# Gate and up slabs as seven block products, with sums of weights by adding DMAs and VectorE, and a down projection in three parts

## The chip, the cores and the metric

The kernel runs on one core of a Trainium2 chip. A core has TensorE (PE, matrix products into the accumulators of PSUM, eight banks), VectorE (DVE), ScalarE (ACT), GpSimd (POOL), and SyncE (SP), which here only issues DMAs. Each engine works through its own list of instructions in order and waits for the others on semaphores. The metric is the device time of one execution in microseconds; lower is better.

## What is computed

One layer of a decoder for 520 tokens (512 of a prompt and 8 that are decoded), width 1024. A feed-forward block stands before and after the mixing part; the change concerns these two blocks ("FFN a" and "FFN b" below). The hidden width is 2816, which is 22 chunks of 128.

```python
D_FF = ((8 * D_MODEL // 3 + 127) // 128) * 128      # 2816

def _swiglu(x, w_gu, w_down):
    gate, up = jnp.split(x @ w_gu, 2, axis=-1)
    return (jax.nn.silu(gate) * up) @ w_down

h = _layernorm(ALPHA * x + 0.5 * _swiglu(x, p['ffa_w_gu'], p['ffa_w_down']), p['ln1_g'], p['ln1_b'])
...
mix = jnp.concatenate([o_da, o_rw], axis=-1) @ p['w_out']
h = _layernorm(ALPHA * h + mix, p['ln2_g'], p['ln2_b'])
y = _layernorm(ALPHA * h + 0.5 * _swiglu(h, p['ffb_w_gu'], p['ffb_w_down']), p['ln3_g'], p['ln3_b'])
```

## The kernel before

Features lie on the 128 partitions and tokens in the columns, so x is 8 chunks (`DC`) of 128x520. Float32 products are made from two parts in the fast format fp32r: a value w is split into w_hi (a rounded copy, by ScalarE) and w_lo = w - w_hi (by VectorE), and each product is hi·hi + hi·lo + lo·hi. So every weight tile of 128x128 costs three matmuls for each half (260 columns) of the tokens.

A **slab** is the weights of one output chunk: 8 tiles of 128x128 for gate and up. It costs 8 tiles x 3 x 2 halves = 48 matmuls of 128x260 (`multiply_slab`, line 298). SyncE loads two slabs at a time, 1 MB, into one of two buffers `RAW` (line 257) when both slabs that lay there are split. ScalarE's `split_high` (line 272) and VectorE's `split_low` (line 279) fill one of four places `WH`/`WL`. Each slab accumulates in one of four sets `acc` of two banks.

`gate_up` is a loop: each pass takes two gate slabs and two up slabs, 4 x 48 matmuls. While TensorE does one pass, ScalarE and VectorE split the slabs of the next (`ahead`), and turn the finished accumulators into two chunks of the hidden vector: silu (line 345), the product (358), and its split into `HH` and `HL` (348, 361). There are 11 passes for the 22 chunks, 2112 matmuls.

`down_tensor` multiplies the whole hidden vector with the down weights: 8 output chunks, each over 22 tiles in four slabs of 6, 6, 5 and 5 tiles (`DOWN_K`), 1056 matmuls. `residual` adds 2·ALPHA·x, taken from its two parts. A LayerNorm follows: its sums are taken by TensorE between the last slabs, and its last chunks become ready one by one while the next stage's first slabs are multiplied (`multiply_halved`, line 854, in FFN b).

TensorE is given work by hand in this order: FFN a, the input projection, the mixing (attention and the recurrent part), the output projection, FFN b. GpSimd has nothing to do in either FFN until the four additions for the norm.

## Time and profile before

| | us |
|---|---|
| median of 3 runs | 1302.99 |
| lowest, highest | 1302.15, 1303.44 |
| span of the profiled execution, first to last instruction | 1303.2 |
| TensorE busy, matmuls | 1253.9 (96%) |
| VectorE busy | 561.9 (43%) |
| ScalarE busy | 422.7 (32%) |
| GpSimd busy | 89.1 (7%) |
| mean granted clock of TensorE | 0.991 |

The profile is of one execution. Its span ends within 0.3 us of the median, so a sum made on the span holds for the median. "Busy" adds up the rows of an engine, and matmul rows overlap each other: the pace of matmuls is read from a stretch and its number of matmuls, not from one row's length. In the same way rows of VectorE and ScalarE can overlap by about 0.1 us, so what an instruction occupies is read from the starts of two that follow each other without idle time.

### The profile page before, as it was taken

How to read it: one execution, taken by the hardware profiler on the slowest of the kernel's cores; microseconds unless marked ns; L12 is line 12 of the kernel's file. 1: busy time of each engine (PE TensorE's matmuls, PEld its weight loads, DVE VectorE, ACT ScalarE, POOL GpSimd, SP SyncE). 2: the span in 40 equal slices, each digit the busy share in tenths (PEclk: the TensorE clock that was granted, in tenths of full speed). 3: DMA queues.
4: the chain of work that ended last, by engine and by line, in shares of the span. 5: the costliest groups of instructions: out<-in, count | busy, mean ns of one | idle time of the engine just before them, and what ended most of it. 6: DMA issues, size and time to landing. Idle time of an engine off the chain costs nothing.

```text
span 1303.2 us, 30892 instructions
## 1 busy us (share of the span) xinstructions
PE 1253.9 (96%) x13258; PEld 1135.4 (87%) x13258; DVE 561.9 (43%) x851; ACT 422.7 (32%) x679; POOL 89.1 (7%) x89
## 2 busy tenths in 40 slices
PE   9999999999999999998878888999999999999996
PEld 8999999999998998886446445698999999999996
DVE  4323333223437543354654544787533333323253
ACT  4222222221223513433543334333422222222223
POOL 0000000000100110000450011010000000000021
PEclk9999999999999999999989999999999999999998
DMA  6222222222222666645644899641222222222221
GB/s 228 98 97 75 86 97 97 69 87 92 83 93 100 243 199 243 223 146 182 210 167 144 283 309 300 244 166 66 98 93 72 93 97 97 80 65 90 90 65 67
DMA packets 57847, 176.96 MB, mean 136 GB/s; under 512 B 7313, under 2 KB 7570, under 8 KB 49426
## 3 DMA queue, kind: packets, MB, share of 16 engines
q1 hardware_dynamic: 54578, 169.48, 38.6%
q10 hardware_dynamic: 3168, 6.02, 1.3%
q8 instruction: 78, 1.28, 0.4%
q14 instruction: 23, 0.19, 0.0%
HBM read 164.64 MB, written 10.83 MB: 135 GB/s over the span
## 4 chain that ended last, share of the span: by engine, by line
PE 86%; DVE 5%; issue 2%; ACT 2%; DMA 2%; POOL 1%; SPq 1%; ACTq 0%; DVEq 0%; POOLq 0%
PE acc L298 66%; PE acc L854 3%; PE acc L1612 2%; PE acc L1682 2%; PE acc L321 2%; PE acc L1164 1%; PE acc L1877 1%; PE acc L545 1%; PE acc L1869 1%; PE acc L1854 1%; PE acc L424 1%; PE acc L1188 1%; DMA scratch<-early_gates 1%; PE acc L411 1%; PE acc L1957 1%
## 5 line engine op out<-in xcount | busy, mean ns | idle before, releaser
L279 DVE TENSOR_TENSOR weights_lo<-weights_raw,weights_hi 128x1024 fp32r<-128x1024 f32 (+2 forms) x184 | 206.6, 1125 | 519.9 <-ACT weights_hi L272 519.8
L272 ACT ACTIVATE weights_hi<-weights_raw 128x1024 fp32r<-128x1024 f32 (+2 forms) x184 | 177.5, 966 | 540.9 <-PE acc L298 519.7
L298 PE MATMUL acc<-x_hi,weights_hi 128*128 128x260 f32 x1696 | 345.0, 285 | 0.1
L298 PE MATMUL acc<-x_hi,weights_lo 128*128 128x260 f32 x1696 | 342.2, 283 | 0.0
L298 PE MATMUL acc<-x_lo,weights_hi 128*128 128x260 f32 x1696 | 342.0, 283 | 0.0
L298 PEld LDWEIGHTS acc<-x_hi,weights_hi 128*128 128x128 f32 x1696 | 262.3, 189 | 12.9 <-issue 11.9
L298 PEld LDWEIGHTS acc<-x_hi,weights_lo 128*128 128x128 f32 x1696 | 262.1, 189 | 0.0
L298 PEld LDWEIGHTS acc<-x_lo,weights_hi 128*128 128x128 f32 x1696 | 261.5, 189 | 0.0
L298 PE MATMUL acc<-hidden_hi,weights_hi 128*128 128x260 f32 x684 | 139.0, 284 | 0.0
L298 PE MATMUL acc<-hidden_hi,weights_lo 128*128 128x260 f32 x684 | 137.7, 283 | 0.0
L298 PE MATMUL acc<-hidden_lo,weights_hi 128*128 128x260 f32 x684 | 137.6, 283 | 0.0
L298 PEld LDWEIGHTS acc<-hidden_hi,weights_hi 128*128 128x128 f32 x684 | 105.4, 188 | 0.9
L298 PEld LDWEIGHTS acc<-hidden_lo,weights_hi 128*128 128x128 f32 x684 | 105.5, 188 | 0.0
L298 PEld LDWEIGHTS acc<-hidden_hi,weights_lo 128*128 128x128 f32 x684 | 105.5, 188 | 0.0
L684 POOL TENSOR_TENSOR scratch<-y_sum 128x520 f32<-128x520 f32 x3 | 5.1, 1698 | 785.2 <-DVE y_sum L449 785.2
L348 ACT ACTIVATE hidden_hi<-scratch 128x520 f32 (+1 forms) x44 | 28.1, 639 | 85.8 <-DVE scratch L358 85.8
L361 DVE TENSOR_TENSOR hidden_lo<-scratch,hidden_hi 128x520 f32 (+1 forms) x44 | 30.8, 700 | 38.9 <-ACT hidden_hi L348 38.9
L1612 PE MATMUL acc<-cache_pages,query_columns 128*32 128x512 f32 x256 | 34.9, 618 | 0.0
L854 PE MATMUL acc<-x_hi,weights_hi 128*128 128x260 f32 x128 | 30.8, 298 | 3.1 <-ACT x_hi L728 1.5
L358 DVE TENSOR_TENSOR scratch<-scratch,acc 128x520 f32<-128x520 f32 x44 | 30.3, 690 | 0.0
L1854 PEld LDWEIGHTS acc<-level_y,inverse_turned 64*64 64x64 f32 x768 | 13.5, 135 | 18.2 <-issue 15.7
L854 PE MATMUL acc<-x_hi,weights_lo 128*128 128x260 f32 x128 | 29.2, 285 | 0.0
(352 smaller groups left out, 1352.8 us busy)
## 6 DMA issues: line engine op xcount, KB each, us to landing
cache_pages<-in_cache_k SPq DMA_DIRECT2D x128, 256.0 KB, 3.6
weights_raw<-in_gate_up_b SPq DMA_DIRECT2D x22, 1024.0 KB, 4.8
weights_raw<-in_gate_up_a SPq DMA_DIRECT2D x21, 1024.0 KB, 4.8
cache_pages<-in_cache_v SPq DMA_DIRECT2D x64, 256.0 KB, 3.6
weights_raw<-in_w_in SPq DMA_DIRECT2D x13, 1024.0 KB, 5.8
projected<-in_cache_v SPq DMA_DIRECT2D x48, 256.0 KB, 3.7
weights_raw<-in_down_a SPq DMA_DIRECT2D x8, 768.0 KB, 4.1
weights_raw<-in_down_b SPq DMA_DIRECT2D x8, 768.0 KB, 4.2
```

The source lines that it names most:

```text
L272: nc.scalar.activation(WH[pr.slot(k)][:, 0:nk, :], RAW[slot][:, 0:nk, P * (k % 2):P * (k % 2) + P], ACT.Copy).then_inc(split_hi, 1)
L279: nc.vector.tensor_tensor(WL[pr.slot(k)][:, 0:nk, :], RAW[slot][:, 0:nk, P * (k % 2):P * (k % 2) + P], WH[pr.slot(k)][:, 0:nk, :].bitcast( ...
L298: mm = nc.tensor.matmul(acc[s][:, a, 0:HALF], w[slot][:, t, :], x[:, k0 + t, HALF * a:HALF * a + HALF], start=begins and t == tiles[0] and ...
L321: mm = nc.tensor.matmul(acc[s][:, a, 0:HALF], w[slot][:, t, :], x[:, t, HALF * a:HALF * a + HALF], start=seen[k] == 1 and m == 0, stop=see ...
L348: nc.scalar.activation(HH[:, bass.ds(2 * (i - 1) + k - 2, 1), :], SCR[:, k:k + 1, :], ACT.Copy).then_inc(h_hi, 1)
L358: dve.tensor_tensor(halves(SCR[:, k, :]), halves(SCR[:, k - 2, :]), accv(k), ALU.mult).then_inc(hidden, 1)
L361: dve.tensor_tensor(HL[:, bass.ds(c, 1), :], SCR[:, k:k + 1, :], HH[:, bass.ds(c, 1), :].bitcast(f32), ALU.subtract).then_inc(acc_free[k], 1)
L411: mm = nc.tensor.matmul(out[32 * q:32 * q + 32, :], MEAN[:, 0:32], x[:, t:t + EIGHTH], start=start, stop=stop)
L854: return nc.tensor.matmul(acc[s][:, h, 0:HALF], w[pr.slot(k)][:, c, :], x[:, c, HALF * h:HALF * h + HALF], start=c == 0 and m == 0, stop=c ...
L1612: mm = nc.tensor.matmul(bank(DECODE_BANK)[32 * h:32 * h + 32, :], QZ[:, h, b, :], PG[k % RING_GROUPS][:, :, P * h:P * h + P], start=b == 0 ...
L1682: mm = nc.tensor.matmul(bank(DECODE_BANK)[32 * j:32 * j + 8, :], WZ[:, n, 8 * b:8 * b + 8], page(N_GROUPS + k, j), start=False, stop=k == ...
L1854: mm = nc.tensor.matmul(two_banks(name)[64 * q:64 * q + 64, r, 64 * k:64 * k + 64], flat(lhs)[rows, cols], flat(rhs)[rows, cols], start=Tr ...
```

## The change

**Seven products.** Of the 22 pairs (gate chunk, up chunk) of each FFN the first two (`PLAIN`) are multiplied as before. Each of the other 20 is seen as a product of 2x2 blocks: the weights as gate or up times the two halves of the 1024 inputs (four quarters of 128x512), x as two halves of the inputs times two halves of the tokens. Such a product is made of seven block products in place of eight, four of them with sums of quarters of weights and of x. One block product is 4 tiles x 3 matmuls = 12 matmuls into one bank (`product_tensor`), a pair 84 where it was 96.

**Sums of x.** Once for each FFN, while TensorE multiplies the two plain pairs, VectorE makes four sums of x of 128x1040 and their low parts, and ScalarE their high parts (`x_sum_vector`, `x_sum_high`, `x_sum_low`). In FFN b x itself lacks its bias in the float32 copy, so ScalarE first makes eight passes of 128x520 (`plain_x_scalar`), which wait until the norm is done. The hidden vector's products use `Y` for the residual, too.

**Sums of weights.** For pair j the three quarters that are used alone are split in one step each (`outer_high`, `outer_low`, 128x1536). The four sums lie in a buffer `SUMS[j % 2]`. SyncE loads two quarters there a second time (2 x 256 KB beside the 1 MB). VectorE writes the two others as sums (`outer_sums_vector`, 128x2x512), and then GpSimd issues two DMAs that add 256 KB within SBUF: [1] += [0], and, after it has landed, [3] += [1] (`whole_sums_pool`). Both must have landed before ScalarE and VectorE split the sums, in two steps of 128x1024 each (`sums_high`, `sums_low`).

**Combining.** The seven results go through ScalarE and VectorE: `first_scalar` (128x260), `second_vector`, `third_vector` (128x260), `ends_vector` (128x520), `gates_vector` (128x780), silu (128x520), `hidden_vector` (128x520), `hidden_high` and `hidden_low`.

**Down in three parts.** The hidden vector is made in groups of 7, 7 and 8 chunks (the first two of them plain), and after each group the down projection over these chunks follows: 8 slabs of 7, 7 or 8 tiles, each result added to `Y` by VectorE (`down_added_vector`). The number of matmuls, 1056, is the same. The last group's slabs are followed by the norm in the order that the output projection had (`out_tensor`, `out_scalar`, `out_vector`). The loops are written out.

The core of the diff:

```diff
-DOWN_K = (6, 6, 5, 5)
+GROUPS = (7, 7, 8)
+GROUP_AT = (0, 7, 14)
+PLAIN = 2
...
+class Sevens:
...
+    ORDER = (1, 6, 7, 5, 2, 4, 3)
...
-DOWN_BODY = [(sum(DOWN_K[:r]), DOWN_K[r], sets, r == 0, r == 3) for sets in ((0, 1), (2, 3)) for r in range(4)]
+DOWN_BODY = [[(0, n, (0, 1), True, True), (0, n, (2, 3), True, True)] for n in GROUPS]
...
+        def plain_x_scalar(act):
+            act.wait_ge(x_ready, DC + 22)
+            for c in range(DC):
+                bias = VEC[:, V_LN + 3 * DC + c:V_LN + 3 * DC + c + 1]
+                nc.scalar.activation(Y[:, c, :], Y[:, c, :], ACT.Identity, bias=bias).then_inc(g("x_passes"), 1)
+        def x_sum_vector(dve, u, n):
+            out = XS[:, n, :, :]
+            if u:
+                dve.wait_ge(g("x_passes"), 4 + DC)
...
+        def outer_sums_vector(dve, sv, j):
+            dve.wait_ge(raw_ready[sv.raw_slot(j)], sv.raw_count(j))
+            raw, to = raw_quarters(sv, j), sums_of(sv, j)
+            two = to[:, :, :].rearrange("p (a b) n -> p a b n", b=2)[:, :, 0, :]
+            nc.vector.tensor_tensor(two, raw[:, 0:2, :], raw[:, 3:4, :].broadcast_to([P, 2, 4 * P]), ALU.add).then_inc(g("summed"), 1)
+        def whole_sums_pool(pool, sv, j):
+            to = sums_of(sv, j)
+            pool.wait_ge(raw_ready[sv.raw_slot(j)], sv.raw_count(j))
+            pool.wait_ge(g("summed"), sv.pair(j) + 1)
+            pool.dma_start(to[:, 1, :], to[:, 0, :], accum_op=ALU.add).then_inc(whole_sums(j), 16)
+            pool.wait_ge(whole_sums(j), whole_count(sv, j) - 16)
+            pool.dma_start(to[:, 3, :], to[:, 1, :], accum_op=ALU.add).then_inc(whole_sums(j), 16)
...
+        def sums_high(act, sv, j, which):
+            at = SUM_AT[which]
+            act.wait_ge(whole_sums(j), whole_count(sv, j))
+            weights_room(act, sv, j)
+            n = 0 if which == "first" else 2
+            nc.scalar.activation(weights_set(j, HI)[:, at:at + 2, :], sums_of(sv, j)[:, n:n + 2, :], ACT.Copy).then_inc(g("parts_hi"), 1)
+        def sums_low(dve, sv, j, which):
+            at = SUM_AT[which]
+            dve.wait_ge(g("parts_hi"), part_done(sv, j, which))
+            n = 0 if which == "first" else 2
+            nc.vector.tensor_tensor(weights_set(j, LO)[:, at:at + 2, :], sums_of(sv, j)[:, n:n + 2, :],
+                                    weights_set(j, HI)[:, at:at + 2, :].bitcast(f32), ALU.subtract).then_inc(g("parts_lo"), 1)
...
+        def sevens_tensor(pe, u, sv, begins):
+            for j in range(sv.pairs):
+                for which in sv.ORDER:
+                    pe.wait_ge(g("parts_lo"), part_done(sv, j, PART_OF[which]))
+                    if begins and j == 0 and which in X_SUM:
+                        pe.wait_ge(g("x_steps"), x_step(u, "low", X_SUM[which]))
+                    if j == 0:
+                        s = BANK_OF[which] // 2
+                        pe.wait_ge(acc_free[s], sv.used0[s])
+                    elif which == 1:
+                        pe.wait_ge(g("evicted"), 2 * sv.pair(j) - 1)
+                    else:
+                        pe.wait_ge(g("combined"), combined_at(sv, j - 1, DRAINED_BY[which]))
+                    product_tensor(pe, sv, j, which)
...
+        def sevens_scalar(act, u, sv, begins, down):
+            last = sv.pairs - 1
+            for j in range(sv.pairs):
+                if j < last:
+                    outer_high(act, sv, j + 1)
+                if j:
+                    silu_scalar(act, sv, j - 1)
+                first_scalar(act, u, sv, j)
+                if j < last:
+                    sums_high(act, sv, j + 1, "first")
+                else:
+                    split_high(act, down, 0, 0)
+                if j:
+                    hidden_high(act, sv, j - 1, begins)
+                if j < last:
+                    sums_high(act, sv, j + 1, "last")
+                else:
+                    for k in (1, 2):
+                        split_high(act, down, 0, k)
+            silu_scalar(act, sv, last)
+            hidden_high(act, sv, last, begins)
+            split_high(act, down, 0, 3)
+        def sevens_vector(dve, u, sv, down):
+            last = sv.pairs - 1
+            for j in range(sv.pairs):
+                if j:
+                    gates_vector(dve, sv, j - 1)
+                if j < last:
+                    outer_low(dve, sv, j + 1)
+                if j:
+                    hidden_vector(dve, sv, j - 1)
+                second_vector(dve, sv, j)
+                if j < last:
+                    sums_low(dve, sv, j + 1, "first")
+                if j:
+                    hidden_low(dve, u, sv, j - 1)
+                third_vector(dve, sv, j)
+                if j == last:
+                    split_low(dve, down, 0, 0)
+                ends_vector(dve, sv, j)
+                if j < last - 1:
+                    outer_sums_vector(dve, sv, j + 2)
+                if j < last:
+                    sums_low(dve, sv, j + 1, "last")
+                else:
+                    for k in (1, 2):
+                        split_low(dve, down, 0, k)
+            gates_vector(dve, sv, last)
+            hidden_vector(dve, sv, last)
+            hidden_low(dve, u, sv, last)
+            split_low(dve, down, 0, 3)
+        def first_down_tensor(pe, u, sv, down, begins):
+            last = sv.pairs - 1
+            def part(t):
+                pe.wait_ge(h_ready, u * FC + sv.chunk0 + sv.pairs - down.body[0][1] + t + 1)
+            for k in range(down.slabs):
+                pe.wait_ge(g("combined"), combined_at(sv, last, ("second", "ends", "gates", "gates")[k]))
+                multiply_slab(pe, down, 0, k, HH, HL, part=part if k == 0 else None)
...
+        def feed_forward_vector(dve, up, u, sevens, downs):
+            sv = sevens[0]
+            x_sum_vector(dve, u, 0)
+            x_sum_vector(dve, u, 1)
+            outer_sums_vector(dve, sv, 0)
+            x_sum_vector(dve, u, 2)
+            x_sum_vector(dve, u, 3)
+            outer_low(dve, sv, 0)
+            sums_low(dve, sv, 0, "first")
+            plain_hidden_vector(dve, up, u, 0)
+            for n in (1, 2):
+                x_sum_low(dve, u, n)
+            plain_hidden_vector(dve, up, u, 1)
+            sums_low(dve, sv, 0, "last")
+            for n in (0, 3):
+                x_sum_low(dve, u, n)
+            for c in range(PLAIN):
+                plain_low_vector(dve, u, c)
+            outer_sums_vector(dve, sv, 1)
+            for n, (sv, down) in enumerate(zip(sevens, downs)):
+                sevens_vector(dve, u, sv, down)
+                if n < 2:
+                    nxt = sevens[n + 1]
+                    for k in range(down.slabs):
+                        down_added_vector(dve, down, 0, k, n == 0)
+                        split_low(dve, down, 1, k)
+                    outer_sums_vector(dve, nxt, 0)
+                    down_added_vector(dve, down, 1, 0, n == 0)
+                    outer_low(dve, nxt, 0)
+                    sums_low(dve, nxt, 0, "first")
+                    down_added_vector(dve, down, 1, 1, n == 0)
+                    sums_low(dve, nxt, 0, "last")
+                    outer_sums_vector(dve, nxt, 1)
+                    for k in (2, 3):
+                        down_added_vector(dve, down, 1, k, n == 0)
...
+            def load_pairs(sv, w):
+                for j in range(sv.pairs):
+                    raw_room(sp, sv.block0 + j)
+                    slot = sv.raw_slot(j)
+                    sp.dma_start(RAW[slot][:, :, :], w[sv.chunk0 + j, :, :].rearrange("p (k n) -> p k n", n=2 * P))\
+                        .then_inc(raw_ready[slot], 16)
+                    wait_from_one(sp, g("parts_lo"), 3 * (sv.pair0 if j < 2 else sv.pair(j - 1)))
+                    for n in (1, 2):
+                        sp.dma_start(sums_of(sv, j)[:, 2 * n - 1, :], w[sv.chunk0 + j, :, 4 * P * n:4 * P * n + 4 * P])\
+                            .then_inc(raw_ready[slot], 16)
...
+            feed_forward_pool(pool, sevens_a)
             norm_pool(pool, 0)
...
+            plain_x_scalar(act)
+            feed_forward_scalar(act, up_b, 1, sevens_b, downs_b)
+            out_scalar(act, downs_b[-1], 2)
```

How the order moves. **VectorE, in the middle of gate and up.** Before, one pass (two chunks; the passes of the loop have the same steps):

```order
L279 TENSOR_TENSOR weights_lo0<-weights_raw0,weights_hi0 128x1024 [waits split_hi,tables_in]
L279 TENSOR_TENSOR weights_lo1<-weights_raw0,weights_hi1 128x1024 [waits split_hi]
L279 TENSOR_TENSOR weights_lo2<-weights_raw1,weights_hi2 128x1024 [waits split_hi]
L358 TENSOR_TENSOR scratch<-scratch,acc2 128x520 [waits slab_used,acc_free0]
L361 TENSOR_TENSOR hidden_lo<-scratch,hidden_hi 128x520 [waits h_hi]
L279 TENSOR_TENSOR weights_lo3<-weights_raw1,weights_hi3 128x1024 [waits split_hi]
L358 TENSOR_TENSOR scratch<-scratch,acc3 128x520 [waits slab_used,acc_free1]
L361 TENSOR_TENSOR hidden_lo<-scratch,hidden_hi 128x520 [waits h_hi]
```

After, one iteration j for one chunk (L652 is `gates_vector` of the pair before, L544 `outer_sums_vector` for the pair after the next, L589 and L579 the low parts for the next pair):

```order
L652 TENSOR_TENSOR scratch<-banks,scratch 128x780 [waits combined,product]
L589 TENSOR_TENSOR weights_lo<-weights_raw1,weights_hi 128x1536 [waits parts_hi]
L660 SCALAR_TENSOR_TENSOR scratch<-scratch 128x520 [waits evicted]
L634 TENSOR_TENSOR scratch<-banks,scratch 128x260 [waits evicted,product]
L579 TENSOR_TENSOR weights_lo<-summed_weights1,weights_hi 128x1024 [waits parts_hi]
L675 TENSOR_TENSOR hidden_lo<-scratch,hidden_hi 128x520 [waits h_hi]
L639 TENSOR_TENSOR scratch<-banks,scratch 128x260 [waits combined,product]
L645 TENSOR_TENSOR scratch<-banks,scratch 128x520 [waits combined,product]
L544 TENSOR_TENSOR summed_weights0<-weights_raw0 128x2x512 [waits raw_ready0]
L579 TENSOR_TENSOR weights_lo<-summed_weights1,weights_hi 128x1024 [waits parts_hi]
```

In place of two 1024-wide splits and two 520-wide steps for each chunk there are ten instructions. The first of the two L579 waits for parts of ScalarE that wait for both adding DMAs (`parts_hi` follows `whole_sums`), and everything behind it stands in VectorE's order, the next `outer_sums_vector` (L544) among it.

**ScalarE beside it**, after, one iteration (L573 is `sums_high`):

```order
L585 ACTIVATE more_weights_hi<-weights_raw0 128x1536 [waits product,raw_ready0]
L656 ACTIVATE scratch<-scratch 128x520 [waits combined]
L629 ACTIVATE scratch<-banks 128x260 [waits h_ready,product]
L573 ACTIVATE more_weights_hi<-summed_weights0 128x1024 [waits product,whole_sums0]
L670 ACTIVATE hidden_hi<-scratch 128x520 [waits combined]
L573 ACTIVATE more_weights_hi<-summed_weights0 128x1024 [waits product,whole_sums0]
```

The first L573 stands ahead of the hidden chunk's high part and waits for `whole_sums`.

**GpSimd and its DMAs.** Before, at the start of the program, GpSimd goes from its constants to the additions of the first norm:

```order
L2786 MEMSET epsilons 128x1 x5
L684 ISA
L684 TENSOR_TENSOR scratch<-y_sum 128x520 [waits early_centred]
L684 TENSOR_TENSOR scratch<-scratch,y_sum 128x520 [waits all_summed,early_centred] x2
```

After, from the same place (the first two pairs of 20 of FFN a):

```order
L3164 MEMSET epsilons 128x1 x5
L551 DMA summed_weights0<-summed_weights0 128x512 [waits summed,raw_ready0]
L553 DMA summed_weights0<-summed_weights0 128x512 [waits whole_sums0]
L551 DMA summed_weights1<-summed_weights1 128x512 [waits summed,raw_ready1]
L553 DMA summed_weights1<-summed_weights1 128x512 [waits whole_sums1]
```

The 20 pairs of DMAs stand where there was nothing; within a pair the second waits for the first to land, and the first for VectorE's sums (`summed`) and the loads. A pair of DMAs for j is issued while TensorE is at pair j-1 or j-2.

## Rows read from the trace of the kernel before

**Rows 1.** The page: the span, and the busy time of each engine.

```profile
span 1303.2 us, 30892 instructions
...
PE 1253.9 (96%) x13258; PEld 1135.4 (87%) x13258; DVE 561.9 (43%) x851; ACT 422.7 (32%) x679; POOL 89.1 (7%) x89
```

**Rows 2.** The chain of waits in order of time: start us, us, what; x matmuls.

```profile
15.50 324.68 PE acc L298 x2700
...
391.05 2.16 PE acc L545 x18
...
924.83 307.11 PE acc L298 x2556
```

**Rows 3.** Timeline of TensorE: start us, us, line, operation; two stage starts.

```profile
9.73 0.39 PE L298 MATMUL acc<-x_lo,weights_hi 128*128 128x260 f32 x2
...
924.67 0.40 PE L298 MATMUL acc<-x_hi,weights_hi 128*128 128x260 f32 x2
```

**Rows 4.** Windows: us, busy us (xcount) of PE, PEld, DVE, ACT, POOL; clock, DMA share, GB/s.

```profile
925.00:1232.00 307.00, 307.00 (x2557) 306.97 (x2556) 101.06 (x113) 81.36 (x102) 0.00 (x0) 1.00 0.28 91
...
1294.00:1296.00 2.00, 0.00 (x0) 0.00 (x0) 2.00 (x5) 1.24 (x3) 2.00 (x2) 0.54 0.44 164
```

**Rows 5.** Timeline of VectorE: durations, and starts of neighbours that follow without idle.

```profile
18.95 2.36 DVE L279 TENSOR_TENSOR weights_lo<-weights_raw,weights_hi 128x1024 fp32r<-128x1024 f32 x2 [3.50 <-ACT weights_hi L272]
...
103.46 1.23 DVE L279 TENSOR_TENSOR weights_lo<-weights_raw,weights_hi 128x1024 fp32r<-128x1024 f32 x1 [2.38 <-ACT weights_hi L272]
...
104.60 0.69 DVE L358 TENSOR_TENSOR scratch<-scratch,acc 128x520 f32<-128x520 f32 x1
...
392.96 0.43 DVE L483 TENSOR_TENSOR y_sum<-acc,y_sum 128x260 f32<-128x260 f32 x1 [1.17 <-PE acc L545]
...
393.30 1.22 DVE L279 TENSOR_TENSOR weights_lo<-weights_raw,weights_hi 128x1024 fp32r<-128x1024 f32 x1
...
883.11 0.70 DVE L456 SCALAR_TENSOR_TENSOR y_sum<-x_lo,y_sum 128x520 f32<-128x520 f32 x1
...
883.73 0.69 DVE L454 SCALAR_TENSOR_TENSOR y_sum<-x_hi,scratch 128x520 f32<-128x520 f32 x1
...
918.25 0.76 DVE L798 SCALAR_TENSOR_TENSOR x_lo<-y_sum,feature_vectors,x_hi 128x520 fp32r<-128x520 f32 x1 [0.80 <-ACT x_hi L728]
```

**Rows 6.** Timeline of ScalarE: the table load, a 1024 copy, a silu, a 520 copy.

```profile
21.66 1.28 ACT L345 ACT_TABLE_LOAD   x1
...
108.07 1.06 ACT L272 ACTIVATE weights_hi<-weights_raw 128x1024 fp32r<-128x1024 f32 x1 [2.02 <-PE acc L298]
...
109.04 0.59 ACT L345 ACTIVATE scratch<-acc 128x520 f32<-128x520 f32 x1
...
99.59 0.64 ACT L348 ACTIVATE hidden_hi<-scratch 128x520 f32 x1 [1.99 <-DVE scratch L358]
```

**Rows 7.** The page: DMA issues, KB each, median us from issue to landing.

```profile
cache_pages<-in_cache_k SPq DMA_DIRECT2D x128, 256.0 KB, 3.6
...
weights_raw<-in_gate_up_b SPq DMA_DIRECT2D x22, 1024.0 KB, 4.8
```

**Rows 8.** The same for the whole program, further issues.

```profile
r_features<-in_cache_v SPq DMA_DIRECT2D x16, 256.0 KB, 4.0
...
out_y<-y_sum SPq DMA_DIRECT2D x8, 260.0 KB, 2.1
...
early_gates<-y_sum ACTq DMA_DIRECT2D x4, 260.0 KB, 2.4
```

**Rows 9.** Timeline of SyncE (SPq issues DMAs), first weight load of the loop.

```profile
15.62 20.38 SPq L257 DMA_DIRECT2D weights_raw<-in_gate_up_a  x4
```

**Rows 10.** Timeline of VectorE and GpSimd, a stretch in which both run.

```profile
349.95 0.96 DVE L279 TENSOR_TENSOR weights_lo<-weights_raw,weights_hi 128x768 fp32r<-128x768 f32 x1 [2.26 <-ACT weights_hi L272]
...
353.56 2.02 DVE L279 TENSOR_TENSOR weights_lo<-weights_raw,weights_hi 128x768 fp32r<-128x768 f32 x1 [1.43 <-ACT weights_hi L272]
...
353.44 1.32 POOL L684 TENSOR_TENSOR scratch<-scratch,y_sum 128x520 f32<-128x520 f32 x1
```

541 lines of the change are left out of this document (345 added, 196 removed).

## The prediction

> **What bounds the kernel now.** I read the page first: TensorE is busy for 1253.9 of 1303.2 us, VectorE for 561.9, ScalarE for 422.7 [rows 1]. The chain of waits shows that each FFN's gate-up and down matmuls are one piece without a gap: 2700 matmuls in 324.68 us and 2556 in 307.11 us [rows 2]. That is 0.1202 us for each in both, so an FFN lasts as long as its matmuls, and taking one away is worth 0.1202 us. In a window of FFN b VectorE works for 101 of 307 us, ScalarE for 81, and the granted clock is 1.00 [rows 4]. Where all matmuls of a stretch go into one bank, as in a block product, 18 take 2.16 us, the same pace [rows 2]. All further steps are times in which TensorE may have to wait in the new order.
>
> **What is removed.** 20 pairs in each FFN cost 84 matmuls for 96: 2 x 20 x 12 = 480, times 0.1202 = **57.7 us less**. One block product is 12 x 0.1202 = 1.44 us, a pair 10.10 us (11.54 before). The down matmuls are the same in number.
>
> **VectorE's steps.** 1024 wide it takes 1.23 us and frees the engine after 1.14 (103.46 to 104.60); 520 wide 0.70 and 0.62; 260 wide from PSUM 0.43 and 0.34 [rows 5]. From 520 to 1024 the slope is 1.05 ns a column, so 1536 costs 1.68, 780 from PSUM 0.88. An iteration (gates 0.88, outer low 1.68, hidden 0.62, second 0.34, first sums low 1.14, hidden low 0.62, third 0.34, ends 0.61, outer sums 1.14, last sums low 1.14) is 8.5 us, under 10.10: VectorE alone isn't the bound. ScalarE has two copies 1024 wide at 1.06, one 1536 wide at 1.49, two 520 and one 260, some 5.2 us [rows 6]. The norm tails and the split of the down slabs (1.2 us of VectorE in each slab of 5.05 us) hide behind matmuls as before; I take 0 for them, and 1 us in all if that fails.
>
> **The loop through the adding DMAs.** What can be longer than 10.10 us is a loop. Let D be the time from the end of the outer sums to the landing of the second adding DMA. From there follow ScalarE's high part (1.06), then on VectorE first sums low (1.14), hidden low (0.62), third (0.34), ends (0.61) and the next outer sums (1.23): with 0.1 for hand-overs the loop takes **P = D + 5.1**. Until D = 5.0 it hides behind a pair; above, each iteration is longer than a pair.
>
> D is not in the trace: GpSimd issues no DMA there. The nearest rows: 256 KB from HBM among other loads land after 3.6 us [rows 7], others after 4.0; 260 KB out of SBUF after 2.1 and 2.4 [rows 8]. The adding DMAs move between places in SBUF like the latter, but read the target too and run beside loads of 1 MB, which take 4.8 us [rows 7], like the former. So D lies between 2 x 2.4 = 4.8 and 2 x 4.0 + 0.2 = 8.2. I see no reason for either end and take the middle of 2.4 and 3.6, 3.0, with 0.1 for each hand-over: **D = 6.2**.
>
> The Trainium skill (DMA: Bandwidth & Descriptors, "Anatomy of one DMA — SWDGE (gpsimd) path") fits a DMA that GpSimd issues as 2.0 us plus bytes over 436 GB/s. By that, an estimate from the page, two of 256 KB are D = 5.2, and the sum below would give 1268; no row here shows such a DMA.
>
> **Cost in groups two and three.** The outer sums of pairs 0 and 1 are made during the down slabs and hide. Count from the group's first block product: the fourth product ends at 5.8, ends and outer sums for pair 2 at 7.65. Then high part and the rest of an iteration bring the last low part of pair 2 at 13.8 + D, and of the last pair p-1 at 13.8 + D + (p-3)(D+5.1) - 1.1. TensorE wants it for the third product of that pair, at 10.10(p-1) + 2.9. The difference is 5D - 30.4 for p = 7 and 6D - 35.4 for p = 8: 0.6 and 1.8 us at D = 6.2. For two FFNs: **4.8 us**.
>
> **Cost in group one** (5 pairs), where nothing was made ahead. FFN a: the block for pair 0 is asked for at 15.62 [rows 9]; VectorE is free of the plain slabs at 18.95 + 2.36 = 21.3 [rows 5], makes two sums of x (1.25 each) and the outer sums, which end at 24.9. High part at 26.0 + D; then on ScalarE a silu and three parts of x (0.5, 3 x 1.0), so the last low part of pair 0 at 31.8 + D. Behind it stand two low parts of x, two hidden parts and the outer sums of pair 1, at 36.4 + D. The last low part of pair 1 follows at 42.0 + 2D, of pair 4 three loops later at 56.2 + 5D, and five products after that the group ends: 63.4 + 5D. Without waits it would end 190 matmuls after 9.73 [rows 3] plus 5 x 10.10: 83.1. **Cost 5D - 19.7 = 11.3 us.** FFN b: x is whole at 918.25 + 0.76 = 919.0 [rows 5]; eight passes of ScalarE (0.64 long, 0.55 apart) [rows 6] end at 923.6, so the outer sums of pair 0 end at 927.3, 902.4 later than in FFN a, and the group at 965.8 + 5D. TensorE is through with the plain pairs at 924.7 already [rows 3], so without waits it would end at 975.2. **Cost 5D - 9.4 = 21.6 us.** (A table load of 1.28 [rows 6] lies in ScalarE's time before, ahead of D's end.) Even with D = 0 TensorE would wait 7.5 us there, since the outer high part comes only after x's passes.
>
> **The sum.** -57.7 + 11.3 + 21.6 + 4.8 = -20.0: 1303.2 becomes **1283**; the median of the runs is within 0.3 us of that span. With all groups waiting the change is 32D - 218.4, so it is zero at **D = 6.8**, and each 0.1 us of D costs 3.2 us.
>
> **Rivals.**
> - **Short DMAs.** D = 5.0, both near the 2.4 us row: groups two and three are free, group one costs 5.3 and 15.6: -36.8, 1266. For it: source and target in SBUF, no HBM. Against: they add, and loads run beside them. The page's fit above speaks for this one.
> - **The adding DMAs are the new bound, and the kernel is slower.** D = 7.7, two at the 3.6 us of the same size with 0.25 of hand-over each. The loop is 12.8 us, longer than the 11.54 of a pair before; +28, 1331. From D = 6.8 on this decides. For it: the row has the same size, and a weight load falls on the second DMA in each loop. In the trace VectorE and GpSimd hinder each other: the split that takes 0.96 alone takes 2.02 beside a GpSimd addition [rows 10]. Against: the row reads HBM. (By the Trainium skill, SBUF — State Buffer, "Who interferes with whom", a tensor_tensor of VectorE takes only the shared read port, so descriptor writing isn't held up; by that the hindrance in the row would be absent and D nothing longer. The row has a GpSimd read, so it doesn't contradict.)
> - **The clock falls in the waits.** At the end of the program the granted clock is 0.54 in a stretch in which TensorE has nothing to do [rows 4]. TensorE waits 7.5 us and more at the start of FFN b and several us in group one of both. If that costs one pair's time at half speed in each FFN, 2 x 10.1, the time is 1303, no change. Against: the forecast's waits are split over several products.
>
> **How the numbers follow.** Forecast (D 5.6 to 6.75) 0.42; short DMAs 0.15; slower 0.35; the clock, or D close to 6.8, 0.08. The measurement can tell about 0.2% (2.6 us) from no change. So faster 0.57, same 0.08, slower 0.35. The range goes from D = 4.8, -38.8 with 2 us off for what I rounded, 1262, to D = 8.2, +44, 1347: I give 1262 to 1345, which leaves out 0.1 at each end or less.
>
> **What would show it.** Right: the matmuls' pace stays 0.120 us; TensorE waits in FFN b's group one for about 20 us, most for weights' low parts; successive outer sums of one group are 11.3 us apart. A group of 5, 7 or 8 pairs in which the outer sums are 10.1 apart shows the short case, 12.5 and more the slower one. The issue-to-landing of the adding DMAs, near 3.0, is the number on which all hangs. The forecast is wrong if TensorE waits for anything else in groups two and three, if VectorE's steps there grow beside GpSimd's work, or if the granted clock in the FFNs falls below 1.

## The result

The changed kernel took **1462.57 us** (median of 4 runs, 1453.69 to 1468.94), the kernel before 1303.22 us beside it: a ratio of **1.121**, 95% interval 1.116 to 1.126. That is slower by 159 us. 1283 was forecast, and the range ended at 1345.

The page of the profile after, the same lines as in [rows 1], and with them the clock in 40 slices and the chain that ended last:

```profile
span 1466.0 us, 30172 instructions
...
PE 1259.5 (86%) x12778; PEld 1123.0 (77%) x12778; DVE 787.6 (54%) x1107; ACT 496.9 (34%) x759; POOL 158.6 (11%) x169
...
PEclk9899989999899999999999999997899899989898
...
PE 39%; DMA 29%; DVE 16%; issue 7%; ACT 5%; SPq 2%; POOL 1%; ACTq 0%; DVEq 0%; POOLq 0%
...
summed_weights<-summed_weights POOLq DMA_DIRECT2D x80, 256.0 KB, 4.5
```

TensorE has its 480 matmuls less (12,778 for 13,258), but the share of the span in which it works fell from 96% to 86%. Before, an FFN was one piece of TensorE in the chain [rows 2]. Now 29% of the chain are DMAs, and the page puts 26% down to `summed_weights<-summed_weights` alone, the 80 adding DMAs. They land after 4.5 us at the median; 3.0 was taken.

The chain of waits inside one group of FFN a (start us, us, what) shows the loop, one turn of it:

```profile
183.93 1.14 DVE summed_weights L544
...
185.11 0.49 issue
185.60 4.42 DMA summed_weights<-summed_weights
190.02 0.28 issue
190.31 5.35 DMA summed_weights<-summed_weights
...
195.68 1.07 ACT weights_hi L573
...
196.77 0.56 DVE weights_lo L579
197.33 0.58 issue
197.91 0.69 DVE hidden_lo L675
198.61 0.35 DVE scratch L639
...
199.05 0.70 DVE scratch L645
199.75 1.14 DVE summed_weights L544
```

From the end of the outer sums (183.93 + 1.14 = 185.07) to the high part (195.68) D is 10.6 us: 0.5 until the first adding DMA begins, 4.4 for it, 0.3, 5.35 for the second. The turn takes 199.75 - 183.93 = 15.8 us, and D + 5.1 = 15.7. So the loop is the one that the prediction drew, step by step; one term of it, D, had been taken 4.4 us too small.

Whom TensorE waits for (us in total, times, longest), kernel after:

```profile
PE banks L603 <- DVE more_weights_lo L579: 68.8, 32, 5.1
PE banks L603 <- DVE weights_lo L579: 67.9, 36, 5.6
PE banks L603 <- issue: 10.0, 2, 5.4
PE banks L603 <- DVE more_weights_lo L589: 8.2, 1, 8.2
```

L579 is the low part of the sums, the last link of the loop: 136.7 us in 68 waits. The 10.0 us to which the view gives no engine are one wait in the first pair of each FFN (4.6 and 5.4). The 8.2 us at L589 are the start of FFN b, put at 7.5.

### The profile page after: what moved, and what is told of

Its sections match the earlier page's. It is cut to its first block, busy times and chain, and to the rows that moved or that the text cites. A ratio compares the mean times of both kernels' runs of the same rounds, so it can differ in the third digit from the quotient of the medians.

```text
span 1466.0 us, 30172 instructions
## 1 busy us (share of the span) xinstructions
PE 1259.5 (86%) x12778; PEld 1123.0 (77%) x12778; DVE 787.6 (54%) x1107; ACT 496.9 (34%) x759; POOL 158.6 (11%) x169
## 4 chain that ended last, share of the span: by engine, by line
PE 39%; DMA 29%; DVE 16%; issue 7%; ACT 5%; SPq 2%; POOL 1%; ACTq 0%; DVEq 0%; POOLq 0%
DMA summed_weights<-summed_weights 26%; PE banks L389 20%; PE banks L603 3%; DVE summed_weights L544 3%; DVE more_weights_lo L579 2%; DVE scratch L645 2%; SPq L3073 2%; ACT more_weights_hi L573 2%; PE banks L1982 2%; PE banks L1239 1%; PE banks L412 1%; DVE hidden_lo L675 1%; ACT weights_hi L573 1%; PE banks L989 1%; PE banks L2052 1%
## 5 line engine op out<-in xcount | busy, mean ns | idle before, releaser
L603 PE MATMUL banks<-x_sums_hi,more_weights_hi 128*128 128x260 f32 x352 | 115.1, 327 | 78.8 <-DVE more_weights_lo L579 68.8
L368 DVE TENSOR_TENSOR weights_lo<-weights_raw,weights_hi 128x1024 fp32r<-128x1024 f32 (+1 forms) x82 | 96.8, 1187 | 118.5 <-ACT weights_hi L360 117.9
L603 PE MATMUL banks<-x_sums_hi,weights_hi 128*128 128x260 f32 x288 | 93.9, 326 | 67.9 <-DVE weights_lo L579 67.9
L579 DVE TENSOR_TENSOR more_weights_lo<-summed_weights,more_weights_hi 128x1024 fp32r<-128x1024 f32 x44 | 53.8, 1222 | 165.9 <-ACT more_weights_hi L573 165.9
L389 PE MATMUL banks<-hidden_hi,weights_hi 128*128 128x260 f32 x576 | 116.5, 283 | 0.0
L389 PE MATMUL banks<-hidden_hi,weights_lo 128*128 128x260 f32 x576 | 115.5, 282 | 0.0
L389 PE MATMUL banks<-hidden_lo,weights_hi 128*128 128x260 f32 x576 | 115.5, 282 | 0.0
L579 DVE TENSOR_TENSOR weights_lo<-summed_weights,weights_hi 128x1024 fp32r<-128x1024 f32 x36 | 44.0, 1222 | 130.3 <-ACT weights_hi L573 130.3
L573 ACT ACTIVATE more_weights_hi<-summed_weights 128x1024 fp32r<-128x1024 f32 x44 | 45.9, 1051 | 192.1 <-DMA summed_weights<-summed_weights 192.1
L603 PE MATMUL banks<-x_sums_lo,more_weights_hi 128*128 128x260 f32 x352 | 110.0, 312 | 0.0
L603 PE MATMUL banks<-x_sums_hi,more_weights_lo 128*128 128x260 f32 x352 | 109.8, 312 | 0.0
L603 PE MATMUL banks<-x_sums_lo,weights_hi 128*128 128x260 f32 x288 | 89.6, 311 | 0.0
L603 PE MATMUL banks<-x_sums_hi,weights_lo 128*128 128x260 f32 x288 | 89.6, 311 | 0.0
L573 ACT ACTIVATE weights_hi<-summed_weights 128x1024 fp32r<-128x1024 f32 x36 | 37.3, 1051 | 144.3 <-DMA summed_weights<-summed_weights 144.3
```

The source lines that it names most:

```text
L368: nc.vector.tensor_tensor(WL[pr.slot(i, k)][:, 0:nk, :], RAW[slot][:, 0:nk, P * (k % 2):P * (k % 2) + P], WH[pr.slot(i, k)][:, 0:nk, :].bi ...
L389: mm = nc.tensor.matmul(acc[s][:, a, 0:HALF], w[slot][:, t, :], x[:, k0 + t, HALF * a:HALF * a + HALF], start=begins and t == tiles[0] and ...
L573: nc.scalar.activation(weights_set(j, HI)[:, at:at + 2, :], sums_of(sv, j)[:, n:n + 2, :], ACT.Copy).then_inc(g("parts_hi"), 1)
L579: nc.vector.tensor_tensor(weights_set(j, LO)[:, at:at + 2, :], sums_of(sv, j)[:, n:n + 2, :], weights_set(j, HI)[:, at:at + 2, :].bitcast( ...
L603: mm = nc.tensor.matmul(product_bank(which), w[a][:, P * t:P * t + P], x[b], start=t == 0 and m == 0, stop=t == 3 and m == 2)
```

## The experiments

Times of the kernel before were 1306.6, 1306.5 and 1307.0 us in the three sets of runs (1299.46 to 1311.48); each ratio is against its own set. In what follows D is read for each of the 40 pairs, from the end of L544 to the first L573 after its second adding DMA, and averaged; in the kernel after it is 10.7 us on average (8.2 to 12.9).

**1. No adding DMA at all.** VectorE makes the third and fourth sum too, from the raw slab, and the second loads go.

```diff
             nc.vector.tensor_tensor(two, raw[:, 0:2, :], raw[:, 3:4, :].broadcast_to([P, 2, 4 * P]), ALU.add).then_inc(g("summed"), 1)
+            dve.wait_ge(g("summed"), n + 1)
+            nc.vector.tensor_tensor(to[:, 1, :], raw[:, 1, :], to[:, 0, :], ALU.add).then_inc(g("summed"), 1)
+            dve.wait_ge(g("summed"), n + 2)
+            nc.vector.tensor_tensor(to[:, 3, :], raw[:, 2, :], to[:, 1, :], ALU.add).then_inc(g("summed"), 1)
```

> All four sums of weights are made by VectorE; the adding DMAs and the second loads of two quarters are gone, the seven products stay. Theory L (the loop from outer sums through two adding DMAs, 10.5 us long, back to outer sums sets the time): nothing is left in that loop, VectorE's iteration grows from 8.5 by two steps 128x512 (0.6 each) to 9.8 us, still under the 10.1 of TensorE; the waits that stay are the starts of the FFNs (about 4 and 14 us) and 0 to 4 us in the groups; so 1303 - 58 + 17 to 22 = 1262 to 1275, successive outer sums of a group 10.1 to 10.6 apart, granted clock in the groups 1.00. Rival V (VectorE has too many steps per pair and its order is what TensorE waits for): more work for it makes it no faster than the changed kernel, above 1450. Rival S (seven products, their bank order or the down projection in three parts cost it): stays above 1330.

Measured: **1267.56 us**, ratio 0.9705 (0.967 to 0.974). VectorE's timeline in a group (start us, us; the lines are one further down than in the listing):

```profile
154.34 1.22 DVE L545 TENSOR_TENSOR summed_weights<-weights_raw 128x1024 f32<-128x1024 f32 x1
155.59 0.69 DVE L547 TENSOR_TENSOR summed_weights<-weights_raw,summed_weights 128x512 f32<-128x512 f32 x1
156.32 0.69 DVE L549 TENSOR_TENSOR summed_weights<-weights_raw,summed_weights 128x512 f32<-128x512 f32 x1
...
164.44 1.22 DVE L545 TENSOR_TENSOR summed_weights<-weights_raw 128x1024 f32<-128x1024 f32 x1
```

The two sums cost VectorE 1.4 us, and the outer sums stand 10.1 us apart, TensorE's own pace of 84 matmuls. So the loss lies in the way in which two sums are made, not in the block products. (The second loads went with the DMAs here; experiment 6 keeps both.)

**2. One adding DMA in place of two.** The third sum goes to VectorE, the fourth stays a DMA, and one of the two second loads goes.

```diff
-            pool.dma_start(to[:, 1, :], to[:, 0, :], accum_op=ALU.add).then_inc(whole_sums(j), 16)
-            pool.wait_ge(whole_sums(j), whole_count(sv, j) - 16)
             pool.dma_start(to[:, 3, :], to[:, 1, :], accum_op=ALU.add).then_inc(whole_sums(j), 16)
```

> One adding DMA for each pair instead of two: VectorE makes the third sum (128x512, 0.6 us), GpSimd adds only the fourth; one 256 KB load less. Theory L: D falls from 10.5 to 4.4 to 5.5 plus 0.5, about 5.6, the loop to 5.6 + 5.1 = 10.7 us, so by the sum 32D - 218 with D = 5.6 to 6 and 0.6 us less for VectorE: 1275 to 1300. Rival V: no faster than 1450. Rival B: half of the gap at most, above 1370.

Measured: **1281.45 us**, ratio 0.9822 (0.977 to 0.9874). The DMA lands after 4.2 us at the median; three successive outer sums stand 11.2 and 12.0 us apart (they start at 159.14, 170.35 and 182.39). In this order of VectorE one DMA of this kind nearly fits behind a pair, two don't.

**3. The same two DMAs, copying and not adding.** This leaves out the two additions.

```diff
-            pool.dma_start(to[:, 1, :], to[:, 0, :], accum_op=ALU.add).then_inc(whole_sums(j), 16)
+            pool.dma_start(to[:, 1, :], to[:, 0, :]).then_inc(whole_sums(j), 16)
```

> The two DMAs of GpSimd copy instead of adding, same bytes, same places, same waits (two of the four sums of weights are then not the sums; this leaves two additions out). If reading the target and adding makes the DMA long: landing 3.2 us and under instead of 4.4 and 5.3, D 7, time about 1340. If it is the queue, GpSimd's 0.86 us and the loads beside it: landing within 0.4 us of 4.4 and 5.3, time within 20 us of 1463.

Measured: **1364.67 us**, ratio 1.0447 (1.0396 to 1.0497). From the chain of waits, the same place as above:

```profile
182.19 2.40 DMA summed_weights<-summed_weights
...
184.87 5.32 DMA summed_weights<-summed_weights
```

Here the first falls from 4.42 to 2.40 us and the second stays at 5.3. Over all 40 pairs the first lands after 2.4 us at the median (4.4 when adding), the second after 4.6 (5.3), and D is 8.2 on average for 10.7. So adding itself is worth some 2.4 us of D, most of it in the first DMA; most of what the second takes has another cause. Neither of the two cases expected is met whole, and the time, 1365, lies between theirs.

**4. The order on VectorE.** The DMAs stay, but the outer sums of pair j+2 are made right after `second_vector` of pair j, one `sums_low`, `hidden_low`, `third` and `ends` earlier.

```diff
                 second_vector(dve, sv, j)
+                if j < last - 1:
+                    outer_sums_vector(dve, sv, j + 2)
                 if j < last:
                     sums_low(dve, sv, j + 1, "first")
...
-                if j < last - 1:
-                    outer_sums_vector(dve, sv, j + 2)
```

> Only one instruction of VectorE's order moves: outer sums for pair j+2 stand ahead of the first low part of the sums of j+1 (was: behind the ends), so they no longer wait for the adding DMAs of j+1. All DMAs stay. Theory L: the loop then spans two iterations, (10.5 + 9) / 2 = 9.8 us each, and what remains is GpSimd's own chain, two DMAs after one another of 10.2 us for a pair, plus whatever the DMAs stretch when they run closer to the loads; period 10.2 to 11.5 instead of 15.7, 28 iterations x 4.5 = 125 us less, some of it not had at the group starts: 1330 to 1370. Rival B (the DMA queues are full: the adds and 1.5 MB of loads for each pair need 15 us whatever the order): no change, above 1440.

Measured: **1305.96 us**, ratio 1.0008 (0.9986 to 1.0031), 24 us under the range of the first theory; its runs spread from 1292.36 to 1313.92, and the profiled one was the fastest, 13.6 us under the median. D is hardly shorter, 10.0 us on average, but in a stretch inside a group (windows: busy us of PE, PEld, DVE, ACT, POOL, granted clock) TensorE doesn't wait:

```profile
160.00:250.00 90.00, 89.41 (x747) 89.20 (x746) 58.28 (x68) 32.95 (x40) 7.78 (x9) 1.00 0.54 158
```

The same 90 us of the kernel after:

```profile
160.00:250.00 90.00, 67.30 (x488) 64.63 (x487) 47.89 (x56) 27.26 (x35) 8.66 (x10) 0.91 0.44 115
```

So it is not D as such that costs, but that `sums_low(j+1)` waits for D and `outer_sums(j+2)` stands behind it. Out of that circle the outer sums no longer wait for the DMAs of the pair before. VectorE's timeline there:

```profile
166.02 1.23 DVE L544 TENSOR_TENSOR summed_weights<-weights_raw 128x1024 f32<-128x1024 f32 x1 [0.60 <-DMA summed_weights<-in_gate_up_a]
...
176.50 1.23 DVE L544 TENSOR_TENSOR summed_weights<-weights_raw 128x1024 f32<-128x1024 f32 x1 [0.52 <-DMA summed_weights<-in_gate_up_a]
178.82 1.23 DVE L579 TENSOR_TENSOR more_weights_lo<-summed_weights,more_weights_hi 128x1024 fp32r<-128x1024 f32 x1 [1.10 <-ACT more_weights_hi L573]
```

The outer sums that end at 167.25 are followed by their first low part at 178.82: 11.6 us, in which D fits. What is left in the profiled run stands almost all in group one of the two FFNs: 8.1 us for L589, 10.9 in two waits without a named engine, and 12.2 of the 19.0 us for L579 (5.9 and 6.3); each of the other waits for L579 is under 1 us.

**5. The group starts.** In the kernel after the outer sums of a group's second pair stand behind both low parts of its first pair, and so behind D.

```diff
+                    outer_sums_vector(dve, nxt, 1)
                     sums_low(dve, nxt, 0, "first")
                     down_added_vector(dve, down, 1, 1, n == 0)
                     sums_low(dve, nxt, 0, "last")
-                    outer_sums_vector(dve, nxt, 1)
```

> The changed kernel with one line moved: where a group of pairs begins behind a down projection, VectorE's outer sums of the group's second pair stand ahead of the low parts of the first pair's sums, not behind them. In the changed kernel they end some 14.9 us after those of the first pair, because they wait for the first pair's two adding DMAs, and in this one some 8 us after. Theory (1462.6 is made of the start, 32 D - 218.4 with D = 10.6, of about 7 us for each of four such group starts, and the rest the lower clock): four starts give back 5 to 7 us each, the time falls by 20 to 28 us, to 1433 to 1443. Rival (the rest over the sum is the lower clock or DMAs that lengthen one another, and the order at the starts costs nothing): under 8 us less, 1455 or more.

Measured: **1441.91 us**, ratio 1.1037 (1.0981 to 1.1092), 20.7 us under the kernel after (23.9 when each is set against the kernel before of its own set). VectorE's timeline, kernel after:

```profile
135.24 1.22 DVE L544 TENSOR_TENSOR summed_weights<-weights_raw 128x1024 f32<-128x1024 f32 x1
148.77 1.23 DVE L579 TENSOR_TENSOR more_weights_lo<-summed_weights,more_weights_hi 128x1024 fp32r<-128x1024 f32 x1 [8.20 <-ACT more_weights_hi L573]
...
151.65 1.22 DVE L544 TENSOR_TENSOR summed_weights<-weights_raw 128x1024 f32<-128x1024 f32 x1
```

and with the line moved:

```profile
138.76 1.22 DVE L544 TENSOR_TENSOR summed_weights<-weights_raw 128x1024 f32<-128x1024 f32 x1
147.62 1.23 DVE L544 TENSOR_TENSOR summed_weights<-weights_raw 128x1024 f32<-128x1024 f32 x1 [3.53 <-DMA summed_weights<-in_gate_up_a]
```

16.4 us between them became 8.9. The same holds at all four starts: the outer sums of the group's third pair, which the prediction put 7.65 us after the first block product, end 15.3, 14.5, 15.5 and 14.6 us after it in the kernel after, and 7.8 us after it in all four with the line moved. Together they were 29 us late. The time gained is less, since D is 10.9 on average in this run and 10.7 in the kernel after.

**6. Both orders at once**, DMAs kept.

> Both reorderings at once, adding DMAs kept: the outer sums of a pair two ahead stand before the first low parts of the next pair (e2_early_sums, 1306.0 us), and at the group starts the second pair's outer sums stand before the first pair's low parts (as e5_border_sums). Theory (time is lost only where the end of the DMAs comes after TensorE's own period; within the groups that is over with the first reordering, and what is left stands at the starts): 5 to 20 us less than e2_early_sums, 1286 to 1301, under the kernel before but over that with all sums by VectorE. Rival (the rest is contention of the DMAs with the loads inside the groups): no change, 1302 to 1308.

Measured: **1288.49 us** (1287.02 to 1290.78), ratio 0.9867 (0.9838 to 0.9895). With all 80 adding DMAs and the second loads in place, the two moves of one line make a kernel that is 12% slower one that is 1.3% faster. Against the medians experiment 6 gains 17 us on experiment 4, against the profiled run of experiment 4 only 5; what the slower runs of that kernel lost no trace shows. In groups two and three of the profiled run here TensorE has no wait of 0.5 us or more; those that are left are in group one.

**7. What lengthens the second DMA.** Only half of each pair's slab is loaded; half of each pair's weights are left out.

```diff
-                    sp.dma_start(RAW[slot][:, :, :], w[sv.chunk0 + j, :, :].rearrange("p (k n) -> p k n", n=2 * P))\
+                    sp.dma_start(RAW[slot][:, 0:4, :], w[sv.chunk0 + j, :, 0:8 * P].rearrange("p (k n) -> p k n", n=2 * P))\
```

> The changed kernel, but the 1 MB load of each pair's slab fetches only its first half (512 KB); the other half keeps what was there, so half of the weights of each pair are left out. Theory (the second adding DMA takes 5.35 us and not 3.3 because the 1 MB load, which starts when the outer low part is done, runs beside it): the second lands after 3.7 to 4.5 us, the first stays at 4.2 to 4.4, the outer sums of successive pairs stand 14 to 14.8 us apart and not 15.6, and the time is 1410 to 1440. Rival (an adding DMA behind another one is slow by itself): 5.2 us or more for the second, and 1450 to 1463.

Measured: **1430.62 us**, ratio 1.0951 (1.0905 to 1.0997). Its chain of waits:

```profile
177.50 4.41 DMA summed_weights<-summed_weights
...
182.20 3.85 DMA summed_weights<-summed_weights
```

In this turn the first is as it was, and the second falls from 5.35 to 3.85. Over all 40 pairs:

| | first lands, median us | second lands, median us | D, average us |
|---|---|---|---|
| kernel after | 4.4 | 5.3 | 10.7 |
| copies (3) | 2.4 | 4.6 | 8.2 |
| half loads (7) | 4.4 | 4.1 | 9.7 |

So half a slab is worth 1.2 us of the second DMA and 1.0 of D: the slab's load runs beside it. In the kernel after SyncE issues, in the turn shown above:

```profile
186.22 0.81 SPq L3050 DMA_DIRECT2D summed_weights<-in_gate_up_a  x2
188.77 0.33 SPq L3046 DMA_DIRECT2D weights_raw<-in_gate_up_a  x1
```

The two second loads fall on the first adding DMA (185.60 to 190.02), the slab's load on its end and, for the most part, on the second (190.31 to 195.66). What the second loads do to the first DMA was not tested by a run. But the last pair of a group has no second loads behind it, and the trace of the kernel after shows it at the end of group one of FFN a (two pieces of the chain of waits, then what SyncE issues from 85 to 100):

```profile
90.53 3.30 DMA summed_weights<-summed_weights
...
94.12 6.14 DMA summed_weights<-summed_weights
```

```profile
93.70 0.33 SPq L331 DMA_DIRECT2D weights_raw<-in_down_a  x1
```

Without a load issued beside it the first DMA takes 3.3 us; the second, beside a load of the down weights, 6.1.

**8. The DMAs alone.** Behind the end of the changed kernel GpSimd issues adds and copies one by one, with nothing beside them.

> The changed kernel with a tail: after every store has landed, GpSimd issues twelve DMAs inside each of two rounds, one at a time, each waiting for the one before: 256 KB added, 256 KB copied, 64 KB added, 64 KB copied, 512 KB added, 512 KB copied, all between quarters of the tiles of sums, with nothing beside them. (Its time is not comparable.) Theory: quiet, 256 KB added land after 3.2 to 3.4 us and copied after 2.2 to 2.4, as the shortest landings in the kernels; about 2 us of it are there whatever the size, so 64 KB still take 1.8 to 2.6 us added, and 512 KB added 4.2 to 5.5. Rival (adding is paid by the byte alone, at twice the copy): 64 KB added under 1.6 us and 512 KB added 6 us or more.

The chain of waits (start us, us from issue to landing), the first six: 256 KB added, copied, 64 KB added, copied, 512 KB added, copied:

```profile
1463.68 3.30 DMA summed_weights<-summed_weights
...
1467.40 2.31 DMA summed_weights<-summed_weights
...
1469.99 2.37 DMA summed_weights<-summed_weights
...
1472.65 1.82 DMA summed_weights<-summed_weights
...
1474.92 4.52 DMA summed_weights<-summed_weights
...
1479.73 2.91 DMA summed_weights<-summed_weights
```

GpSimd's timeline of an adding one and a copy (start us, us of issuing, idle before):

```profile
1469.99 0.86 POOL L3182 DMA_DIRECT2D summed_weights<-summed_weights  x1 [2.01 <-DMA summed_weights<-summed_weights]
1472.65 0.56 POOL L3182 DMA_DIRECT2D summed_weights<-summed_weights  x1 [1.80 <-DMA summed_weights<-summed_weights]
```

From one start to the next, 0.3 to 0.5 us of hand-over included, means of four (three for the copy of 512 KB, since nothing follows its last one):

| KB | added, us | copied, us |
|---|---|---|
| 64 | 2.7 | 2.2 |
| 256 | 3.6 | 2.7 |
| 512 | 4.8 | 3.2 |

A straight line through 64 and 512 KB gives 2.4 us and 1.2 for each 256 KB when adding, 2.0 and 0.6 when copying. So adding doubles the share that goes by bytes and puts 0.4 us on the fixed one; the issue on GpSimd is 0.3 us longer (0.86 us for 0.56). By this line two thirds of an adding DMA of 256 KB do not depend on its size, and the rival, under which 64 KB would take less than 1.6 us, is out.

The Trainium skill (DMA: Bandwidth & Descriptors, "Anatomy of one DMA — SWDGE (gpsimd) path") gives 2.0 us plus bytes over 436 GB/s, which is 2.6 for 256 KB and 3.2 for 512. From one start to the next the copies here agree with it (2.7 and 3.2); from issue to landing they take 0.3 us less (2.3 and 2.9). The adding ones are longer than the page's figure either way, and the section has no other figure for them.

**9. The two sums on GpSimd as additions**, no DMAs and no second loads.

```diff
-            pool.dma_start(to[:, 1, :], to[:, 0, :], accum_op=ALU.add).then_inc(whole_sums(j), 16)
+            pool.tensor_tensor(to[:, 1, :], raw[:, 1, :], to[:, 0, :], ALU.add).then_inc(g("pool_summed"), 1)
...
-            pool.dma_start(to[:, 3, :], to[:, 1, :], accum_op=ALU.add).then_inc(whole_sums(j), 16)
+            pool.tensor_tensor(to[:, 3, :], raw[:, 2, :], to[:, 1, :], ALU.add).then_inc(g("pool_summed"), 1)
```

> The third and fourth sum of each pair by GpSimd's own additions of 128x512 from the raw slab, no adding DMAs and no second loads. Before, GpSimd took about twice VectorE's time for one addition, so some 1.2 us each: D about 3 us, under the 6 us at which the loop's period falls to TensorE's own. Theory (what costs in the changed kernel is the time between the outer sums and the last sum alone, whoever makes it): as with all sums by VectorE, 1260 to 1275. Rival (GpSimd's additions and VectorE's hinder one another, so that VectorE's steps in the groups grow): 1280 to 1310.

Measured: **1268.87 us**, ratio 0.9706 (0.9672 to 0.974), as fast as all four on VectorE. GpSimd and VectorE do hinder each other. GpSimd's timeline, then VectorE's:

```profile
167.85 2.22 POOL L551 TENSOR_TENSOR summed_weights<-weights_raw,summed_weights 128x512 f32<-128x512 f32 x1 [6.66 <-DVE summed_weights L545]
170.15 1.30 POOL L553 TENSOR_TENSOR summed_weights<-weights_raw,summed_weights 128x512 f32<-128x512 f32 x1
```

```profile
167.69 1.22 DVE L579 TENSOR_TENSOR more_weights_lo<-summed_weights,more_weights_hi 128x1024 fp32r<-128x1024 f32 x1
...
170.78 2.28 DVE L589 TENSOR_TENSOR weights_lo<-weights_raw,weights_hi 128x1536 fp32r<-128x1536 f32 x1 [0.61 <-ACT weights_hi L585]
```

The first addition starts beside VectorE's low part and takes 2.22 us instead of 1.30; VectorE's outer low part starts beside the second addition and takes 2.28 instead of 1.75. By the Trainium skill (SBUF — State Buffer, "Who interferes with whom") a VectorE instruction with two SBUF inputs contends with GpSimd's reads, and the shared port is an exclusive lock, so one of the two stands until the other is through. The rows agree: they overlap by 1.06 and 0.67 us, and the one that came second is 0.9 and 0.5 us longer. All of it hides here: D is some 4 us, and neither engine is the bound.

**10. The better version pushed on.** All sums on VectorE as in 1; in FFN b the first pair's sums and its outer high and low part are made before the sums of x, in the time in which VectorE waits for the passes over x, and some parts of the sums of x change places with those of the weights.

```diff
+            outer_high(act, sevens_b[0], 0)
             plain_x_scalar(act)
...
+            if u:
+                outer_sums_vector(dve, sv, 0)
+                outer_low(dve, sv, 0)
             x_sum_vector(dve, u, 0)
```

> The kernel with all four sums by VectorE (e1_all_vector, 1267.6 us), and in the second feed forward the first pair's sums and its high and low outer parts are made while VectorE waits for the bias passes over x (5.1 us idle there), ahead of the x sums and not behind them. Theory (TensorE's 8.5 us wait and the 3.1 us at the second pair stand behind VectorE's row of steps, 4.4 us of which move into the idle time and 2 more are no longer ahead of the second product): 4 to 9 us less, 1259 to 1264. Rival (the wait is then for the x sums and their parts, which have to come behind the passes in any order): under 2 us less, 1265.5 to 1268.

Measured: **1260.65 us** (1258.37 to 1269.29), ratio **0.9661** (0.9627 to 0.9695): 7 us less than in 1, the fastest of all and 3.4% under the kernel before. (The two intervals overlap; what supports the gain is the waits in the trace.) TensorE's wait of 8.5 us for the first product is gone. It now waits 1.8 us for the first and 3.5 for the second:

```profile
899.30 0.36 PE L608 MATMUL banks<-x_hi,more_weights_hi 128*128 128x260 f32 x1 [1.78 <-ACT scratch L516]
904.51 0.39 PE L608 MATMUL banks<-x_sums_hi,more_weights_hi 128*128 128x260 f32 x1 [3.53 <-DVE more_weights_lo L584]
```

## Why the prediction was wrong

**What held.** A matmul costs 0.1202 us: in the stretch of experiment 4, 747 of them fill 90 us, 0.1205 each. VectorE's steps are what was read off before: the low part of 1024 columns, the one beside which GpSimd issues its first DMA, has a mean of 1.22 us on the page. The loop is P = D + 5.1 (15.8 measured at D = 10.6). The start of FFN b waits 8.2 us (7.5). The mechanism that decided is the second rival, put at 0.35: the adding DMAs as the new bound.

**The step that failed** is "I see no reason for either end and take the middle": D = 6.2, with 8.2 as the upper end. The loop was right and its term D was too small: D is 10.7, beyond the upper end. In the runs it is made of:

- the DMA by itself, 3.3 us quiet for 256 KB added, where 3.0 was taken: twice 0.3;
- the company of loads: the first lands after 4.4 at the median, beside the next pair's second loads, the second after 5.3, beside the slab. Together some 3 us, the largest part. For the second it is shown by a run, half a slab takes 1.2 us off its median (experiment 7); for the first only by rows, 3.3 us where no load is beside it;
- hand-overs of 0.5 and 0.3 us where 0.1 was taken.

There were reasons for the upper end, and beyond, in the rows that stood there: the prediction itself said that the DMAs "read the target too and run beside loads of 1 MB". So the 2.1 and 2.4 us of plain writes out of SBUF could only be a lower end, and a middle between them and a load in company was no estimate for a transfer that adds and is in company too. The 4.0 us per DMA at the upper end came from plain loads of 256 KB, so it was no bound for one that adds beside a load of 1 MB.

**A second term was missing.** In groups two and three the prediction let the outer sums of pairs 0 and 1 hide and counted from pair 2. The rows of experiment 5 show up to which D that holds. The outer sums of pair 0 end at 136.46 and the group's first block product starts at 153.04, 16.6 us later. Those of pair 1 end D + 5.2 behind those of pair 0, and those of pair 2 D + 4.6 behind those of pair 1, so they end 2D - 6.8 after the first product. The prediction had them at 7.65, which needs D under about 7.2: true at its 6.2, no longer at its own upper end. At the D of 11.2 and 10.9 there they come 7.6 us late, and 29 us together at the four starts. Put beside what D gives by 32D - 218.4 (us against the kernel before in the same set):

| kernel | D | by the sum | measured |
|---|---|---|---|
| after | 10.7 | +124 | +159 |
| group starts mended (5) | 10.9 | +130 | +135 |
| half loads (7) | 9.7 | +92 | +124 |
| copies (3) | 8.2 | +45 | +58 |

With the starts mended the old sum is right within 5 us; without, it misses some 30 us where D is 9.7 or more, and 13 for the copies, where D is anything from 5.5 to 12.4 and its average says less. So the 179 us between forecast and result are 32 x 4.5 = 144 from D and about 30 from the starts, with some 5 left over. With the right D alone the sum would have said 1427.

The same by groups, from the profiled run of the kernel after: the time from a group's first block product to the end of its last, less 10.10 us for each pair, and what the prediction's formula gives for that group at D = 10.7 (us).

| group | FFN a: 1 | 2 | 3 | FFN b: 1 | 2 | 3 |
|---|---|---|---|---|---|---|
| measured | 30.3 | 31.6 | 40.4 | 42.3 | 33.7 | 38.7 |
| by the formula | 33.8 | 23.1 | 28.8 | 44.1 | 23.1 | 28.8 |

(The 42.3 hold the 8.2 us before the first product.) Group one, which has no such start, comes out 2 to 4 us under the formula; the four others 8 to 12 over it. The measured row adds up to 217.0; less 57.7 that is 159.3, of the 162.8 us by which the two profiled spans differ.

**The clock.** It fell in the waits as the third rival said, within the groups too: in 184 to 190 it is 0.50, the lower of its two levels (1.2 GHz), and TensorE puts only 19 matmuls into 3.98 us. Before that it had waited 3.8 us (until 182.23), and it waited 2.0 more inside the stretch. In the down projection ahead of the group, 133 to 153, it has no wait and the clock is 1.00.

```profile
184.00:190.00 6.00, 3.98 (x19) 3.75 (x18) 5.69 (x6) 0.92 (x2) 0.86 (x1) 0.50 0.52 118
...
133.00:153.00 20.00, 20.00 (x170) 20.00 (x169) 9.52 (x10) 4.35 (x4) 1.72 (x2) 1.00 0.52 161
```

It adds little: the loop's turn has no matmul in it (it goes DMA, ScalarE, VectorE), so slower matmuls only fill part of the wait, and outside the groups the profiled span is 3.5 us longer in all. How much of the few us left over is the clock's was not separated.

**What a better forecast needed.** Not D more exactly, but a look at how steep the result is in D: 32 us for each us, with 0.6 us of D between forecast and break-even, and a term measured nowhere in the trace. A range from 1262 to 1345 said too little of that: with D up to 10.7 and the starts it would have reached past 1450.

## What to carry to other kernels

A DMA in a chain that comes round once per tile costs its full latency each time; count the turn (here D + 5.1 us against 10.1 of TensorE) and first look whether the order on the waiting engine can break the circle, since one line moved was worth 157 us here while D stayed near 10. Work of 0.7 us on an engine that has room (VectorE was busy for 54%) wasn't worth handing to a transfer that takes 4 to 5 us: even with both lines moved the kernel with the DMAs stays 21 us behind the one with all sums on VectorE. Where a duration isn't in the trace, take the nearest rows in the same company as lower end, add what the new transfer reads besides and what runs beside it, and check the formula's own assumptions again at the upper end.
